# Prompt heads in pairs beside a sample sequence, and the prompt's gate and output tiles between scores and values

## What is computed

```
proj = h @ w_in;  q, k, v, g = split(proj, 4)        # q, k rms-normed by head
prompt:  o = softmax(q k^T / sqrt(128) - slope * distance, causal) v      # 8 heads, 256 x 256
sample s: k_all = cache_k[page_table[s]] (8 pages of 128 rows) and 4 new; the same for v
          of 4 cached blocks of 256 rows, the 3 with the highest q . mean(k) take part
          o = softmax(scores of these and the new rows) v
out = (o * silu(g)) @ w_out;   y = x + gate(c) * out
```

## Time and profile before

| | |
|---|---|
| median of 3 runs | 760.6 us (759.21 to 764.26) |
| the profiled execution | 760.23 us |
| its span, first to last instruction | 758.4 us |
| mean granted TensorE clock | 0.95 |
| PE busy | 656.5 us, 87% |
| DVE busy | 353.9 us, 47% |
| ACT busy | 221.8 us, 29% |
| POOL busy | 196.5 us, 26% |
| moved by DMA | 191.62 MB, 253 GB/s over the span |

### The profile page before, as it was taken

The page is one execution under the profiler, slowest core; times in us unless marked ns, Lnnn a source line. Parts: engine busy times, 40 slices in busy tenths (PEclk is TensorE's granted clock), DMA queues, the critical chain, the costliest instruction groups (busy, mean ns, idle before and its releaser), DMA issues.

```text
span 758.4 us, 9813 instructions
## 1 busy us (share of the span) xinstructions
PE 656.5 (87%) x3616; PEld 363.3 (48%) x3616; DVE 353.9 (47%) x648; ACT 221.8 (29%) x464; POOL 196.5 (26%) x221
## 2 busy tenths in 40 slices
PE   3859999999999999999998899998775787666797
PEld 1237746666674764343342567774332333333342
DVE  2252646547465563532106224227656834574512
ACT  1334244423524432110003354434321223123000
POOL 0014127036033412200000579984110101010000
PEclk9969999999999999999999999999988889788899
DMA  9994337873883897389937442556899795989901
GB/s 331 363 391 168 112 111 247 317 240 118 327 281 118 319 326 286 126 291 325 341 111 268 182 142 89 214 173 236 331 381 372 301 405 202 384 309 392 399 15 62
DMA packets 82443, 191.62 MB, mean 253 GB/s; under 512 B 4167, under 2 KB 12359, under 8 KB 82268
## 3 DMA queue, kind: packets, MB, share of 16 engines
q1 hardware_dynamic: 80796, 184.84, 66.8%
q0 software_dynamic: 1264, 4.98, 1.8%
q10 hardware_dynamic: 336, 1.18, 0.4%
HBM read 168.57 MB, written 22.41 MB: 252 GB/s over the span
## 4 chain that ended last, share of the span: by engine, by line
PE 75%; DVE 7%; DMA 5%; SPq 5%; ACT 4%; issue 4%; POOL 0%; DVEq 0%; ACTq 0%; POOLq 0%
PE bank L635 18%; PE bank L643 9%; PE bank L879 7%; PE bank L607 7%; PE bank L626 5%; DMA ring<-in_cache_k 4%; PE bank L821 3%; PE bank L840 3%; PE bank L667 3%; PE bank L674 3%; PE bank L582 3%; PE bank L662 2%; PE bank L712 2%; SPq L552 2%; DVE arena L1582 2%
## 5 line engine op out<-in xcount | busy, mean ns | idle before, releaser
L460 POOL TENSOR_TENSOR weights_low<-ring,weights_high 128x512 fp32r<-128x512 f32 x80 | 100.5, 1300 | 61.0 <-PE bank L626 61.0
L635 PE MATMUL bank<-weights_high,h_high 128*128 128x512 f32 x288 | 115.3, 400 | 0.0
L635 PE MATMUL bank<-weights_high,h_low 128*128 128x512 f32 x288 | 113.3, 393 | 0.0
L995 ACT ACTIVATE weights_high<-ring 128x1024 fp32r<-128x1024 f32 x72 | 73.5, 1051 | 86.4 <-PE bank L643 86.4
L1582 DVE STREAM_TRANSPOSE arena<-ring 128x1024 f32<-128x1024 f32 x64 | 73.8, 1213 | 36.4 <-DMA ring<-in_cache_k 36.4
L643 PE MATMUL bank<-weights_low,h_high 128*128 128x512 f32 x288 | 85.0, 396 | 0.0
L635 PEld LDWEIGHTS bank<-weights_high,h_high 128*128 128x128 f32 x288 | 54.0, 188 | 27.6 <-issue 15.9
L959 ACT ACTIVATE partial<-bank 128x512 f32<-128x512 f32 x40 | 23.6, 590 | 136.9 <-PE bank L662 58.0
L635 PEld LDWEIGHTS bank<-weights_high,h_low 128*128 128x128 f32 x288 | 54.2, 188 | 12.0
L674 PE MATMUL bank<-consts,arena 128*128 128x128 f32 x232 | 37.7, 298 | 24.9 <-ACT arena L1012 12.4
L643 PEld LDWEIGHTS bank<-weights_low,h_high 128*128 128x128 f32 x288 | 53.5, 188 | 11.6
(11 more groups left out here) (184 smaller groups left out, 861.5 us busy)
## 6 DMA issues: line engine op xcount, KB each, us to landing
ring<-in_cache_k SPq DMA_DIRECT2D x64, 512.0 KB, 7.0
ring<-in_cache_v SPq DMA_DIRECT2D x64, 512.0 KB, 7.1
ring<-in_w_ada SPq DMA_DIRECT2D x12, 2048.0 KB, 11.5
ring<-in_w_ret_in SPq DMA_DIRECT2D x8, 2048.0 KB, 9.7
ring<-in_state_ret SPq DMA_DIRECT2D x32, 512.0 KB, 7.7
out_state_sample<-ring SPq DMA_DIRECT2D x32, 512.0 KB, 5.6
ring<-in_w_moba_in SPq DMA_DIRECT2D x8, 2048.0 KB, 11.2
ring<-in_w_ret_in SPq DMA_DIRECT2D x8, 1024.0 KB, 14.1
```

Source lines behind the costliest of these rows:

```text
L460: tensor_tensor(w_low[:, slot, k, :], ring[:, slot, k * CH:(k + 1) * CH], high[:, k, :].bitcast(F32), ALU.subtract).then_inc(low_ready[LOW ...
L635: pe.matmul(o[i][:, :], xs[p][i][:, k, :], high[:, k, :], start=k == 0 and p == 0, stop=False)
L995: nc.scalar.activation(w_high[u[0] == "moba"][:, 2 * i:2 * i + 2, :].rearrange("p a b -> p (a b)"), w[:, 2 * i * CH:(2 * i + 2) * CH], ACT ...
```

## The change

Prompt heads no longer come one to a sequence. HEAD_EARLY (1, 2, 4, 6) stand beside sequences 0 to 3 where one stood before. HEAD_LATE (3, 5, 7) have their scores and maximum at the end of sequences 1, 2 and 3, after the values, and their values at the start of the next sequence, ahead of the sample scores. All heads are turned by sequence 4.

Gate chunk 7: its first prompt tile and its sample tile come after the values of sequence 1, the second prompt tile between scores and values of sequence 2, the turning of GT in sequence 3. Its weights come in the stream after the pages of sequence 1 instead of 3.

The output: tile 0 of chunk 1 stands between scores and values of sequence 5, tile 1 of chunk 1 in 6, both prompt tiles of chunk 0 in 7. Behind the values of 7 there are only the two sample tiles. The weights of chunk 1 go to the space of the prompt's turned queries and keys, and SP issues them ahead of the keys of sequence 5, when the scores of head 7 are done. The turned prompt heads take the space of the gate rows that they have used up, and the output's products go to two spare buffers. DVE adds each tile to x at the end of its sequence. POOL gates two heads in sequences 0, 2 and 3, one in 1 and 4.

In the diff, bank_plan's edits are left out (they repeat the order of PE).

```diff
 ADA_AT = {RH - 1: [(0, c) for c in ADA_GATE]}
-G_AFTER = 3
+
+
+HEAD_EARLY = (1, 2, 4, 6)
+HEAD_LATE = {1: 3, 2: 5, 3: 7}
+
+GATE_TILE = {0: (6, 1), 2: (7, 1)}
+GATE_AFTER = {1: (7, 0)}
+GATE_TURN = 3
+LAST_OUT_AT = 5
+OUT_TILES = {5: ((1, 0),), 6: ((1, 1),), 7: ((0, 0), (0, 1))}
...
             units.append(("v", s, 1))
-        if s == G_AFTER:
+        if s in GATE_AFTER:
             units.append(("moba", 7, 0))
     return units
+
+
+def heads_to_turn(s):
+
+    if s == 0:
+        return (0,)
+    return HEAD_EARLY[s - 1:s] + ((HEAD_LATE[s - 1],) if s - 1 in HEAD_LATE else ())
...
-        w_last = L1["kt"].rearrange("p a b -> p (a b)")[:, 0:KT * CH].rearrange(
-            "p (k n) -> p k n", k=KT)
-        pyT = pqT
+        w_last = mod[:, 0:2, :, :].rearrange("p a b c -> p (a b c)").rearrange("p (k n) -> p k n", k=KT)
+
+        out_tmp = (squares, norm_b[:, CH:2 * CH])
...
+                if (kind, a, b) == ("k", LAST_OUT_AT, 0):
+
+                    wait_full(sp, ("pS", MH - 1))
+                    sp.dma_start(w_last, t["w_moba_out"][0].rearrange("(k p) n -> p k n", p=P)[:, :, CH:2 * CH]
+                                 ).then_inc(w_last_in, 16)
                 if n >= RING:
                     released(n - RING)
...
-            wait_full(sp, ("QK", NS - 1))
-            sp.dma_start(w_last, t["w_moba_out"][0].rearrange("(k p) n -> p k n", p=P)[:, :, CH:2 * CH]
-                         ).then_inc(w_last_in, 16)
...
             prompt_values(0)
             for s in range(NS):
-                if s + 1 < MH:
-                    prompt_scores(s + 1)
-                if s == NS - 1:
-                    for h in (s - 1, s):
-                        head_turned(h)
-                    for h in (s - 1, s):
-                        wait_read(pe, ("pY", h))
+                if s - 1 in HEAD_LATE:
+                    prompt_values(HEAD_LATE[s - 1])
+                if s < len(HEAD_EARLY):
+                    prompt_scores(HEAD_EARLY[s])
                 sample_scores(s)
-                if s == NS - 1:
-                    prompt_tile(("mout", 0), pyT, 0)
-                if s == 0:
-                    g_chunk(6, (1,))
-                if s:
-                    sequence_turned(s - 1)
-                if s + 1 < MH:
-                    prompt_values(s + 1)
-                if 0 < s < NS - 1:
-                    head_turned(s - 1)
-                sample_values(s)
-                if s == G_AFTER:
-                    g_chunk(7, range(2))
+                if s in GATE_TILE:
+                    g_chunk(GATE_TILE[s][0], GATE_TILE[s][1:])
+                if s == GATE_TURN:
                     for half in range(2):
                         wait_read(pe, ("row", "moba", 6 + half, 2))
                         turn(("GT", half), [L1["G"][:, 2, (4 * half + j) * P:(4 * half + j + 1) * P]
                                             for j in range(4)])
-
-            prompt_tile(("mout", 0), pyT, 1)
+                for c, n in OUT_TILES.get(s, ()):
+                    for h in HEAD_EARLY[-1:] + (MH - 1,):
+                        wait_read(pe, ("pY", h))
+                    prompt_tile(("mout", c), lambda k, n: L1["G"][:, n, k * P:(k + 1) * P], n)
+                if s:
+                    sequence_turned(s - 1)
+                if s < len(HEAD_EARLY):
+                    prompt_values(HEAD_EARLY[s])
+                for h in heads_to_turn(s):
+                    head_turned(h)
+                sample_values(s)
+                if s in GATE_AFTER:
+                    g_chunk(GATE_AFTER[s][0], GATE_AFTER[s][1:])
+                if s in HEAD_LATE:
+                    prompt_scores(HEAD_LATE[s])
+
             sequence_turned(NS - 1)
-            prompt_tile(("mout", 1), pyT, 0)
             pe.wait_ge(yTs_ready, 1)
-            sample_tile(("mout", 0))
-            prompt_tile(("mout", 1), pyT, 1)
-            add_groups(("mout", 0))
-            sample_tile(("mout", 1))
-            add_groups(("mout", 1))
+            for c in range(2):
+                sample_tile(("mout", c))
+                add_groups(("mout", c))
...
-                read_out(nc.scalar.activation(pyT[:, h, :], o[:, 0:NP], ACT.Copy), ("pY", h))
+
+                read_out(nc.scalar.activation(L1["G"][:, 0:2, h * DH:(h + 1) * DH],
+                                              o[:, 0:NP].rearrange("p (n m) -> p n m", n=2), ACT.Copy), ("pY", h))
...
             prompt_rows(0)
             for s in range(NS):
-                if s + 1 < MH:
-                    prompt_exps(s + 1)
-                if s == NS - 1:
-                    head_turned(s - 1)
-                    head_turned(s)
+                if s - 1 in HEAD_LATE:
+                    prompt_turned(HEAD_LATE[s - 1])
+                    prompt_rows(HEAD_LATE[s - 1])
+                if s < len(HEAD_EARLY):
+                    prompt_exps(HEAD_EARLY[s])
+                if s in GATE_TILE:
+                    c, n = GATE_TILE[s]
+                    gate_values(c, (n,) if n == 0 else (n, 2))
+                if s == GATE_TURN:
+                    for half in range(2):
+                        label = ("GT", half)
+                        o = wait_full(act, label)
+                        read_out(nc.scalar.activation(GT[:, 4 * half:4 * half + 4, :],
+                                                      o[:, :].rearrange("p (k m) -> p k m", k=4)[:, :, 0:32],
+                                                      ACT.Copy), label)
                 if s:
                     sequence_turned(s - 1)
-                if s + 1 < MH:
-                    prompt_turned(s + 1)
-                if 0 < s < NS - 1:
-                    head_turned(s - 1)
+                if s < len(HEAD_EARLY):
+                    prompt_turned(HEAD_EARLY[s])
+                for h in heads_to_turn(s):
+                    head_turned(h)
...
-                if s == 0:
-                    gate_values(6, (1, 2))
-                if s + 1 < MH:
-                    prompt_rows(s + 1)
-                if s == G_AFTER:
-                    gate_values(7, range(3))
-                    for half in range(2):
-                        label = ("GT", half)
-                        o = wait_full(act, label)
-                        read_out(nc.scalar.activation(GT[:, 4 * half:4 * half + 4, :],
-                                                      o[:, :].rearrange("p (k m) -> p k m", k=4)[:, :, 0:32],
-                                                      ACT.Copy), label)
+                if s < len(HEAD_EARLY):
+                    prompt_rows(HEAD_EARLY[s])
+                if s in GATE_AFTER:
+                    gate_values(GATE_AFTER[s][0], (GATE_AFTER[s][1],))
+                if s in HEAD_LATE:
+                    prompt_exps(HEAD_LATE[s])
...
-                    pool.wait_ge(py_ready, 2 * (s - 1))
...
-                h = s
-                wait_read(pool, ("pO", h))
-                for n in range(2):
-                    wait_read(pool, ("row", "moba", 6 + h // 4, n))
-                    nc.gpsimd.tensor_tensor(py[h % 2][:, n, :], py[h % 2][:, n, :],
-                                            L1["G"][:, n, h * DH:(h + 1) * DH], ALU.mult).then_inc(py_ready, 1)
+                heads = (0,) if s == 0 else ()
+                if s - 1 in HEAD_LATE:
+                    heads += (HEAD_LATE[s - 1],)
+                if s < len(HEAD_EARLY):
+                    heads += (HEAD_EARLY[s],)
+                for h in heads:
+                    wait_read(pool, ("pO", h))
+                    for n in range(2):
+                        wait_read(pool, ("row", "moba", 6 + h // 4, n))
+                        nc.gpsimd.tensor_tensor(py[h % 2][:, n, :], py[h % 2][:, n, :],
+                                                L1["G"][:, n, h * DH:(h + 1) * DH], ALU.mult).then_inc(py_ready, 1)
+                gated += len(heads)
+                if heads:
+                    pool.wait_ge(py_ready, 2 * gated)
...
-                    tmp = h_rows[:, n, cs]
+                    tmp = h_rows[:, n, cs] if tag[0] == "rout" else out_tmp[n if n < 2 else c]
                     read_out(nc.vector.tensor_tensor(tmp, o[:, :], mod[:, 2, n // 2, cs], ALU.mult), label)
                     wait_read(dve, label)
                     ins = nc.vector.tensor_tensor(X[:, n, cs], X[:, n, cs], tmp, ALU.add)
-                    if c == 1:
+                    if c == ends:
                         ins.then_inc(x_done, 1)
...
+                    if pg == 3 and s - 1 in HEAD_LATE:
+                        prompt_sums(HEAD_LATE[s - 1])
                 if s == 0:
                     prompt_sums(0)
                 if s:
                     output_rows(s - 1)
-                if s + 1 < MH:
-                    prompt_max(s + 1)
+                if s < len(HEAD_EARLY):
+                    prompt_max(HEAD_EARLY[s])
...
-                if s + 1 < MH:
-                    prompt_sums(s + 1)
```

(51 more changed lines are left out.)

20 lines of the change are left out of this document (10 added, 10 removed).

## The result

The changed kernel takes 781.9 us (median of 4 runs, 779.2 to 783.9) against 762.0 us before (4 runs): 1.025 times as long, 95% interval 1.022 to 1.029. The profiled span is 782.2 us, 23.8 more than before, and the mean granted clock 0.935 instead of 0.95. There are as many matmuls and as many bytes; PE is busy 5.3 us longer, the other engines within 3 us of before. What changed is the order. The traced execution is the slowest of the four.

The account below looks back on a forecast made before the run. The last 245 us bound the kernel, a chain of page landing, transposes, scores and values. Span 758.4 plus 34.0 late at the last values minus 17.8 gained in the tail gave 774.6, time 776; 8 in 10: 760 to 783.

Parts of the forecast that it names:

- the calendar: Step-by-step sum of sequences 0 to 7 and the tail: 776 us; 770 to 784 given 0.62.
- signs of being wrong: Scores(4) ending before 655, transposes of sequences 2 and 4 still waiting for DMA, or last values ending before 745 us.
- The point from which the sign decides: End of the last values: later than 17.8 us after 727.0 the change loses, earlier it wins.
- Covered by v(0,1), which lands later: Sequences 0 and 1: silu and gating ahead of the exponentials cost nothing; values(1) still end at 569.2 us.
- Values 2: Sequence 2: tile ends at 603.5, first transpose at 611.5, values end at 618 us, 22 late.
- Sequence 3: Keys issued at 611.4 land by 625.6, then transposes and scores: scores end at 636.4 us against 601.7.
- come back next: After sequence 3, where 35 us are lost, the gate chunk's 18.4 us (616.2 to 634.6) are regained.
- Values with a tile ahead of them: Sequences 5 to 7: scores end to first transpose 9.1 us behind one tile, then 5.5 to the values' end.
- The tail: After the last values: 13.6 us against 31.4 before, so 17.8 gained.
- The clock did not stay up: Rival: filled waits keep PE warm, four scores take 4.1 us, 8.4 us go: 768 us; 762 to 770 given 0.15.
- repaid: Rival: pages wait in the ring, later steps shorten from 23 towards 18 us: 762 to 766; 756 to 767 given 0.13.
- the stream hides all: Rival: the 71 MB transfer stream is the true limit and hides both new waits: 749 us; 745 to 756 given 0.08.

Follow-up runs that it names:

- Runs 1 to 3: Changed kernel with late heads' scores issued ahead of the values (777.8 us), with gate chunk 7 whole behind values of sequence 1 (779.9 us), and with both (763.4 us).
- Run 9: Changed kernel with both edits of Runs 1 to 3, head 3's exponentials ahead of gate copies, and head 0 turned one sequence later: 755.7 us.
- run 2: Changed kernel with both prompt tiles of gate chunk 7 behind the values of sequence 1, none between scores and values of 2: 779.9 us.

## Why the prediction was right

**The mechanism.** The forecast was slower by 16 us with the calendar as the likeliest case; measured are about 20. Its two causes, DVE's prompt_max behind the values and v(2,1) behind the gate tile, are there with the waits that were named: 20.6, 20.9 and 10.3 us at prompt_max (said: 20, 18, 10) and 31.6 us at the gate tile (said: over 25). The transfers stood still for 20 of these 31.6 us, not for all: from 576 to 584 they ran at 408 GB/s. None of the forecast's signs of being wrong occurred: scores(4) ended at 672.5, the transposes of sequences 2 and 4 waited for no page, the last values ended at 766.8. Runs 1 to 3 show that they are the cause and that they are one behind the other: together they are 18 us, and either alone hides the removal of the other. The point from which the sign decides, 17.8 us at the end of values(7), was passed by 22. Of the 7.6 us by which the traced span exceeds the 774.6, 3.0 are there at scores(7), 2.8 come in values(7) and 1.8 in the tail.

**Sequences 0 and 1: a term put at nothing.** "Covered by v(0,1), which lands later" was wrong. The exponentials of sequence 0 came behind the silu copies, POOL's gating and a change of ScalarE's table, the first transpose at 545.5 instead of 540.9, and scores(1) started 2.8 late. Values(1) ended 3.4 us after the forecast's 569.2, and that carries on to scores(2). Run 9 shows the place to be worth 0.6 to 0.8%, in a kernel without the two waits.

**Values 2: an undersized term.** From the end of the gate tile (606.9) to the first transpose (616.8) it took 9.9 us, where I had 8.0 (603.5 to 611.5). ScalarE's timeline shows most of what was missing:

```profile
607.10 1.28 ACT L1174 ACT_TABLE_LOAD   x1 [10.61 <-PE bank L899]
608.39 1.08 ACT L1174 ACTIVATE arena<-bank 128x512 f32<-128x512 f32 x2
...
613.72 1.28 ACT L1225 ACT_TABLE_LOAD   x1
615.01 0.41 ACT L1225 ACTIVATE arena<-arena,stats 128x64 f32<-128x64 f32 x1
```

Two table loads, not one, lie on the path: one for the silu, which didn't start until the tile was there, and one back for the exponentials; the sum had only the second. The values that follow took 7.7 (616.8 to 624.5), where I had 6.5. With the 3.5 by which scores(2) were later already, values(2) end 6.5 after the forecast.

**Sequence 3: near the forecast, by another limit.** I had the landing of the keys set scores(3) and prompt_max just not. With values(2) at 624.5 it was prompt_max again (625.4 plus its 1.1 plus 9.2 of transposes gives 635.7). The wait bit three times out of three, and in run 2, with its pages there in time, DVE still waited 48.1 us at prompt_max.

**Sequences 4 to 7.** The steps hold: the scores are late by 33.6, 27.4, 35.4 and 30.1, each with 3 to 4 us carried from above. In sequence 7 DVE's add_to_x did stand ahead of the transposes. One sentence of the prediction doesn't fit its own calendar: the gate chunk's 18.4 us were to "come back next", but the calendar's lateness falls only from 34.7 to 29.5 there, since DVE's wait stands in the way. Measured are 39.9 to 33.6.

**The end.** Values with a tile ahead of them were priced at 5.5 us from the first transpose on, from one row. They took 5.5 in sequence 5 (granted clock 1.00), 7.2 in 6 (0.76) and 8.4 in 7 (758.3 to 766.8, clock 0.60), where it counted. With 2.9 us in sequence 7 this is the largest miss of a term that the sum has. The tail took 15.4 where 13.6 were forecast, its first sample tile 3.49 (clock 0.55) instead of 1.9:

```profile
769.16 3.49 PE L908 MATMUL bank<-ring,h_turned 128*32 128x512 f32 x16 [0.75 <-DVE h_turned L1666]
```

**The rivals.** The clock did not stay up where the calendar had idle time. Scores took 6.4, 5.7, 5.5 and 5.4 us in sequences 2, 3, 4 and 6, at a granted clock of 0.63, 0.71, 0.73 and 0.75; in sequences 5 and 7, after waits of 1.7 and 1.5 us, they took 4.1 at 1.00. The mean over the span is lower than before. The rule of the Trainium skill (TensorE: Matmul & The Clock Gate, "HAM oscillation — how this bites in real kernels") that waits for data between bursts bring the engine down holds in this trace at its 3.8 to 8.5 us waits before the four slow scores. Filled gaps kept the clock up for some of the values behind them, not for the scores, whose idle time stayed.

Of the lateness at scores(3), 6.3 us were repaid by scores(4) and 6.2 more by (5). It grew by 8.0 to (6) and fell by 5.3 to (7), 9.8 repaid in all, but the end of values(7) is 39.8 late again. That the stream hides all is refuted by the 20 us without a transfer.

## What to carry to other kernels

Filling an engine's gap pays in full only if everything the filler's helpers add to the other engines' queues is ready when they reach it: ask, for each instruction put last in a queue, who produces its input and what stands behind it. In a ring of buffers, a buffer's last user sets the start of the load that comes one turn later and of everything queued behind that; moving a tile late moves those loads late. And when two waits cover each other, undoing either alone shows almost nothing (here 0.7 and 0.2% against 2.3%); try both before calling a cause refuted.

## What the runs showed of the hardware that was not expected

ScalarE's change of table is not always hidden in a wait. Before the load at 618.83 came 5 us ahead of the tile that its silu waited for. In the changed kernel the load at 607.10 came only when the tile was there, after 10.6 us of idle time, and cost its 1.28 us on the path; a second one at 613.72 led back to the exponentials. What makes the difference was not tried.

The same pause between the same kinds of instructions left the clock at either level. Before, a tile of 7 us, a pause of 4 us with few matmuls, and the values of sequence 7; after, 14 us of tiles, the same pause and the values. The windows of the two (columns as in the earlier trace rows), first before:

```profile
712.00:719.00 7.00, 7.00 (x24) 3.10 (x17) 3.94 (x19) 0.00 (x0) 0.00 (x0) 1.00 1.03 397
719.00:723.00 4.00, 1.28 (x12) 0.67 (x13) 1.38 (x2) 2.50 (x15) 0.00 (x0) 1.00 0.55 205
723.00:727.00 4.00, 4.00 (x73) 1.99 (x72) 0.00 (x0) 0.00 (x0) 0.00 (x0) 1.00 0.00 0
```

and after:

```profile
742.00:756.00 14.00, 14.00 (x40) 6.14 (x33) 5.33 (x21) 0.00 (x0) 0.00 (x0) 1.00 0.79 315
756.00:760.00 4.00, 1.28 (x11) 0.78 (x13) 1.38 (x2) 2.50 (x15) 0.00 (x0) 0.84 0.32 131
760.00:767.00 7.00, 6.76 (x72) 2.51 (x72) 0.16 (x1) 0.00 (x0) 0.00 (x0) 0.60 0.01 2
```

PE was busy for 1.28 us of the 4 in both, yet one stayed at 2.4 GHz (granted clock 1.00) and the other was at 1.2 GHz for most of the values (0.60 on average). One tile or two is not the difference. Run 9 has the same two tiles and the same pause, and its values ran at the full clock:

```profile
718.88 14.00 PE L899 MATMUL bank<-ring,arena 128*128 128x512 f32 x32
...
734.90 0.44 PE L850 MATMUL bank<-consts,arena 128*128 128x128 f32 x2 [1.91 <-ACT arena L1222]
...
736.38 3.64 PE L860 MATMUL bank<-ring,arena 128*8 128x256 f32 x64 [0.81 <-issue]
```

What decides it is not shown. A single sequence's price behind a tile (5.5 us before, 8.4 after) is therefore not a safe term of a sum.
